# Gated DeltaNet heads: u and w no longer formed, each scan step solves with the transposed chunk inverse; decays in one orientation from rounded pairs

## The reference

```
G = cumsum(g);  decay[i,j] = exp(G_i - G_j) for i >= j
A = strictly_lower((beta k) k^T * decay)
u = (I + A)^-1 (v * beta);   w = (I + A)^-1 (k * beta * exp(G))
qk = (q k^T) * decay;  k_dec = k * exp(G_last - G)
for each chunk:
    v_new = u - w S
    o = (q exp(G)) S + qk v_new
    S = S * exp(G_last) + k_dec^T v_new
```

## Time and profile before

| | us |
|---|---|
| median of 3 runs | 2143.46 |
| lowest, highest | 2142.41, 2148.03 |
| span of the profiled execution | 2142.6 |

### The profile page before, as it was taken

How to read it: one execution, slowest core, us unless ns; L and a number is a source line. 1 busy time by engine, 2 the same in 40 slices (tenths; PEclk the granted TensorE clock), 3 DMA queues, 4 the chain that set the end, 5 groups by cost and what they waited for, 6 DMA issues and landing times. The chain is left out here.

```text
span 2142.6 us, 40127 instructions
## 1 busy us (share of the span) xinstructions
PE 1958.1 (91%) x15035; PEld 1587.5 (74%) x15036; DVE 1106.7 (52%) x1759; ACT 770.8 (36%) x1255; POOL 422.2 (20%) x332
## 2 busy tenths in 40 slices
PE   6899999999999989999999989899998998899990
PEld 3888888888886558887788866777776776677770
DVE  3446656656656464322322348555457557554338
ACT  2523423423432112221222202554446546543332
POOL 0154144245144031221111233100000000000004
PEclk7999999999999999999999999999999999999995
DMA  8042242243233532234322513875658758755354
GB/s 287 30 142 72 76 142 85 71 134 97 84 111 116 185 119 98 89 101 131 99 98 94 190 49 128 307 257 167 203 178 300 234 175 309 239 166 167 105 177 162
DMA packets 186864, 320.12 MB, mean 149 GB/s; under 512 B 26137, under 2 KB 77729, under 8 KB 186619
## 3 DMA queue, kind: packets, MB, share of 16 engines
q1 hardware_dynamic: 170683, 286.00, 40.8%
q10 hardware_dynamic: 12192, 17.00, 2.3%
q0 software_dynamic: 3744, 13.63, 1.8%
HBM read 283.89 MB, written 32.67 MB: 148 GB/s over the span
## 5 line engine op out<-in xcount | busy, mean ns | idle before, releaser
L1216 PE MATMUL pp<-whi,xTh 128*128 128x512 f32 (+1 forms) x1152 | 443.5, 385 | 22.4 <-issue 12.4
L1910 ACT ACTIVATE whi<-wring 128x1024 fp32r<-128x1024 f32 (+1 forms) x324 | 314.7, 979 | 411.2 <-PE pp L1218 353.6
L1218 PE MATMUL pp<-wlo,xTh 128*128 128x512 f32 (+1 forms) x1152 | 430.7, 374 | 0.0
L1217 PE MATMUL pp<-whi,xTl 128*128 128x512 f32 (+1 forms) x1152 | 429.9, 373 | 0.0
L2536 DVE TENSOR_TENSOR wlo<-wring,whi 128x1024 fp32r<-128x1024 f32 (+1 forms) x180 | 209.5, 1164 | 270.8 <-ACT whi L1910 222.7
L1216 PEld LDWEIGHTS pp<-whi,xTh 128*128 128x128 f32 x1152 | 218.0, 189 | 70.9 <-issue 27.8
L1218 PEld LDWEIGHTS pp<-wlo,xTh 128*128 128x128 f32 x1152 | 217.5, 189 | 38.9
L1217 PEld LDWEIGHTS pp<-whi,xTl 128*128 128x128 f32 x1152 | 218.3, 190 | 34.6
L1216 PE MATMUL pp<-whi,hTh 128*128 128x512 f32 x528 | 212.7, 403 | 7.8 <-DVE hTl L2558 2.8
L1218 PE MATMUL pp<-wlo,hTh 128*128 128x512 f32 x528 | 207.0, 392 | 0.0
L1217 PE MATMUL pp<-whi,hTl 128*128 128x512 f32 x528 | 206.6, 391 | 0.0
(11 more groups left out here) (321 smaller groups left out, 3065.5 us busy)
## 6 DMA issues: line engine op xcount, KB each, us to landing
wring<-in_moe_w_gu SPq DMA_DIRECT2D x320, 256.0 KB, 3.8
wring<-in_ada_w SPq DMA_DIRECT2D x80, 512.0 KB, 4.9
wring<-in_moe_w_down SPq DMA_DIRECT2D x160, 256.0 KB, 3.5
wring<-in_ffn_w_gu SPq DMA_DIRECT2D x80, 256.0 KB, 3.0
wring<-in_dn_w_in SPq DMA_DIRECT2D x128, 128.0 KB, 3.1
wring<-in_ffn_w_down SPq DMA_DIRECT2D x40, 256.0 KB, 2.9
expert_in<-zeros SPq DMA_DIRECT2D x36, 256.0 KB, 3.3
wring<-in_ada_w SPq DMA_DIRECT2D x32, 256.0 KB, 5.3
```

The costliest lines, as they stand in the source:

```text
L1216: pe.matmul(out, hi[:, c0 + c, tt], wh, start=(first and c == 0), stop=False)
L1217: pe.matmul(out, lo[:, c0 + c, tt], wh, start=False, stop=False)
L1218: mm = pe.matmul(out, hi[:, c0 + c, tt], wl, start=False, stop=(last and c == nk - 1))
L1910: act.activation(whi[:, hs, 0:nk, 0:w], wring[:, ring_v.slot(k), 2 * s:2 * s + nk, 0:w], ACT.Copy)\
```

## The change

u and w are no longer formed. With X = (I + A)^-1 diag(beta), a step is now: right side v - exp(G) (k S) on DVE (`right_sides`), solve X times that on PE (`solve`, one f32 product for each direction), copy to `vnew` on ACT (`new_values`), then the adds as before. beta goes into the decay (the bias of Exp) of the transposed A and into the decayed keys (`EKB`), so POOL's right sides go. Step 0 solves with v itself, and `reads` multiplies the transposed keys `kT` (two buffers now) with the state. Direction d uses `xinv[:, 1 - d]`.

The decays of both uses now come from one product in one orientation: the gates are split into a rounded high and a low part (`g_high`, `G_LOW`), POOL masks both (`span_high`, `span_low`, four operations instead of two), and PE multiplies them with a strict triangle in fp32r, 384 and 256 columns, high and low each, summed in PSUM. One Exp with log beta serves both A and the weights: `decay_w` and its Exp go, and `weights` waits for the blocks of A. At level 5 of the inverse half of the x products are not needed, and the inverse is kept as `xinv` instead of transposed.

The order changes on every engine. In the new scan the decays of head h + 1 come first (ACT's Exps before `new_values(1)` and behind it), then keys and Gram products, and the Silu of q and v between `new_values` 2, 3 and 4; before, ACT had the Silus first and the Exps behind them. On DVE the taps of the v convolution are spread over the steps. In POOL's block the causal weights, decayed keys and masks move among the level masks. Ahead of head 0 ACT does the Exps right behind the Silu of q. The core of the diff, without renamed buffers and semaphore counts:

```diff
 # PE
-            def decay_a(h, d): ...
-            def decay_w(h, d): ...
+            def decay(h, i):
+                if h == 0 and i == 0:
+                    pe.wait_ge(S["mask_ready"], 2)
+                    pe.wait_ge(S["gate_act"], 6)
+                pe.wait_ge(S["gm_ready"], 4 * h + 2 * i + 2)
+                if i:
+                    pe.wait_ge(S["qkn"], h + 1)
+                for part in (slice(0, 3 * P), slice(3 * P, NT)):
+                    out = PP[3 - i][:, part] if part.start == 0 else PP[3 - i][:, 512:512 + NT - 3 * P]
+                    pe.matmul(out, strict_mask[:, i, :], span_high[:, i, part], start=True, stop=False)
+                    mm = pe.matmul(out, strict_mask[:, i, :], span_low[:, i, part], start=False, stop=True)
+                mm.then_inc(S["decay_ps"], 1)
...
-                    for b in range(2):
+                    for b in ((1, 0) if n == 10 else (0, 1)):
                         for d in range(2):
                             p = halves(b)
+                            if n == 10 and b == d:
+                                continue
...
+            def solve(h, k):
+                for d in range(2):
+                    t = tile_of(k, d)
+                    if k == 0:
+                        pe.wait_ge(S["v_ready"], h + 1)
+                        pe.wait_ge(S["inv_upd"], h * 24 + upd_count(13 - d))
+                    else:
+                        pe.wait_ge(S["rhs_ready"], h * 8 + (2 * (k - 1) + d + 1))
+                        pe.wait_ge(S["o_upd"], h * 18 + 4 * (k - 1) + (4 if k == 1 else 2))
+                    if k == 1:
+                        pe.wait_ge(S["sp_ready"], h * 2 + (d + 1))
+                    pe.matmul(add_bank(d)[:, 2 * P:3 * P], xinv[:, 1 - d, t, :], rhs[:, d, :] if k else v_of(h)[:, tiles(t)],
+                              start=True, stop=True).then_inc(S["solve_ps"], 1)
...
 # scan(h) on PE now, in order (early: output units of the last head; the rest of h + 1 only if there is one)
+  solve(h, 0)   reads(h, 1)   early(0, 1)   decay(h + 1, 0)    adds(h, 0)   early(1, 2)
+  solve(h, 1)   early(2, 3)   decay(h + 1, 1)   adds(h, 1)     early(3, 4)
+  k_columns(h + 1)   reads(h, 2)   early(4, 5)   solve(h, 2)   early(5, 6)
+  gram_k(h + 1)      adds(h, 2)    early(6, 7)   reads(h, 3)   early(7, 8)
+  gram_q(h + 1)      solve(h, 3)   early(8, 9)   adds(h, 3)    early(9, 10)
+  v_tokens(h + 1)    reads(h, 4)   early(10, 11) solve(h, 4)   early(11, 12)   adds(h, 4)
 # ahead of head 0 on PE now
+  project(0, 24, 27)  decay(0, 0)  decay(0, 1)  project(0, 27, 29)  k_columns(0)  project(0, 29, 30)
+  gram_k(0)  project(0, 30, 32)  gram_q(0)  v_tokens(0)
 # POOL
-                for d, m in enumerate((GT, LT)):
-                    pool.tensor_tensor(per_tile(gm[:, d, :]), mat_bc(m), col_bc(gcol(G_, d, h)), ALU.mult)\
+                for i, m in enumerate((GE, LE)):
+                    for dst, col in ((span_high, g_high[...].bitcast(F32)), (span_low, gcol(G_LOW, 1 - i, h))):
+                        pool.tensor_tensor(per_tile(dst[:, i, :]), mat_bc(m), col_bc(col), ALU.mult)\
...
 # ACT
+            def decays(h, i):
+                act.wait_ge(S["decay_ps"], 2 * h + i + 1)
+                if h and i == 0:
+                    act.wait_ge(S["wm_step"], 2 * h)
+                d = 1 - i
                 for t in range(T):
+                    at = t * P if t < 3 else 512 + (t - 3) * P
+                    ins = act.activation(ex[:, i, t * P:(t + 1) * P], PP[3 - i][:, at:at + P], ACT.Exp,
                                          bias=gates5[:, LB, t, h + 8 * d:h + 8 * d + 1])
...
+                def new_values(k):
+                    for d in range(2):
+                        act.wait_ge(S["solve_ps"], h * 10 + (2 * k + d + 1))
+                        if h or k:
+                            act.wait_ge(S["s_add_ps"], h * 10 + 2 * (k - 1) + (d + 1))
+                        act.activation(vnew[:, d, :], add_bank(d)[:, 2 * P:3 * P], ACT.Copy).then_inc(S["vn_ready"], 1)
 # scan(h) on ACT now, in order
+  k_squares(h + 1)  new_values(0)  state_new of both d  decays(h + 1, 0)  new_values(1)  store of the state
+  decays(h + 1, 1)  k_columns(h + 1)  new_values(2)  grams(h + 1, 0)  conv_silu(h + 1, 1)  new_values(3)
+  grams(h + 1, 1)  conv_silu(h + 1, 2)  new_values(4)  v_tokens(h + 1)  q_squares(h + 1)  chunk_high  out_square(h)
 # ahead of head 0 on ACT now
+  k_squares(0)  conv_silu(0, 1)  decays(0, 0)  decays(0, 1)  k_columns(0)  grams(0, 0)  conv_silu(0, 2)  grams(0, 1)
+  z_silu(0)  v_tokens(0)  q_squares(0)
 # DVE
+                        dve.scalar_tensor_tensor(rhs[:, d, :], read_bank(d)[:, 0:P], gates5[:, MINUS_EG, t, h + 8 * d:h + 8 * d + 1],
+                                                 v_of(h)[:, tt], ALU.mult, ALU.add).then_inc(S["rhs_ready"], 1)
 # scan(h) on DVE now, in order; right_sides(k) also scales q S, conv(a) is tap a of v of head h + 1
+  k_sums(h + 1)  right_sides(1)  outputs(0)  k_normal(h + 1)  conv(0)  new_states(1)  outputs(1)  conv(1)
+  right_sides(2)  conv(2)  new_states(2)  outputs(2)  conv(3)  right_sides(3)  a_blocks(h + 1, 0)
+  new_states(3)  outputs(3)  conv(4)  right_sides(4)  a_blocks(h + 1, 1)  outputs(4)
```

More of the change, by code:

```diff
@@ L211, in backbone @@
         scratch = sb("scratch", [P, 15388])
+        strict_mask = sb("strict_mask", [P, 2, P], F32R)
+        g_high = sb("g_high", [P, T, 16], F32R)
         ctx.close()
@@ L1066, in scan @@
-                pe.wait_ge(S["kdec_ready"], h * 2 + 2)
-                pe.wait_ge(S["wm_step"], h * 2 + 2)
-                pe.wait_ge(S["wt_sb"], h * 2 + 2)
-                adds(h, 0)
-                early(0, 2)
+                solve(h, 0)
+                reads(h, 1)
+                early(0, 1)
+                if nx:
+                    decay(h + 1, 0)
+                adds(h, 0)
+                early(1, 2)
+                solve(h, 1)
+                early(2, 3)
+                if nx:
+                    decay(h + 1, 1)
@@ L1071, in scan @@
+                adds(h, 1)
+                early(3, 4)
                 if nx:
                     k_columns(h + 1)
-                reads(h, 1)
-                early(2, 3)
+                reads(h, 2)
+                early(4, 5)
+                solve(h, 2)
+                early(5, 6)
                 if nx:
                     gram_k(h + 1)
-                adds(h, 1)
-                early(3, 5)
+                adds(h, 2)
+                early(6, 7)
+                reads(h, 3)
+                early(7, 8)
@@ L1527, in _ @@
                     k_decayed(h, d)
+                for n in range(8, 10):
+                    off_mask(h, n)
                 for n in range(10, 12):
@@ L1841, in scan @@
                     act.wait_ge(S["state_out"], h * 32 + 1)
-                    act.activation(state_new[:, d, :], bank(2 * d + 1)[:, 0:P], ACT.Copy).then_inc(S["sp_ready"], 1)
+                    act.activation(state_new[:, d, :], add_bank(d)[:, 0:P], ACT.Copy).then_inc(S["sp_ready"], 1)
+                if nx:
+                    decays(h + 1, 0)
+                new_values(1)
                 for d in range(2):
@@ L2396, in scan, with outputs @@
+                def outputs(k):
+                    for d in range(2):
+                        t = tile_of(k, d)
+                        tt = slice(t * P, (t + 1) * P)
+                        out = add_bank(d)[:, P:2 * P]
                         dve.wait_ge(S["s_add_ps"], h * 10 + (2 * k + d + 1))
@@ L2417, in scan @@
-                    if nx and k == 0:
-                        conv(h + 1, 2, 2, 5)
-                assert n_o == 18
+                            dve.wait_ge(S["o_upd"], h * 18 + done[0])
+                            o_step(dve.tensor_tensor(oacc[:, tt], oacc[:, tt], out, ALU.add))
+                if nx:
+                    k_sums(h + 1)
+                right_sides(1)
+                outputs(0)
+                if nx:
+                    k_normal(h + 1)
+                if nx:
+                    conv(h + 1, 2, 0, 1)
@@ L2421, in _ @@
+                if nx:
+                    conv(h + 1, 2, 4, 5)
+                right_sides(4)
+                if nx:
+                    a_blocks(h + 1, 1)
+                outputs(4)
+                assert done[0] == 18
             for part in range(2):
```

373 lines of the change are left out of this document (168 added, 205 removed).

## The result

The changed kernel takes 2153.78 us (median, 2147.57 to 2162.93) against 2142.55 us (2137.57 to 2148.03) of the kernel before on the same chip: ratio 1.0056, interval 1.0044 to 1.0069. It is slower by 0.56%, 12 us; the prediction said 2135. The profiled execution has a span of 2148.2 us against 2142.6.

A forecast was written before the change was run, and what follows sets the result against it. PE, busy 91%, was first suspect, but in the scan the chain through DVE and ACT queues was to decide. 2142.6 - 8.5 - 2 - 3 = 2129.1 of span, 2130 as median; clock falls of 5 made 2135, range 2120 to 2150.

The forecast's parts named there:

- part 1: PE work in a scan falls by 5.6 us to 15.1, with both decays taking 1.2 us.
- more than 1.2: Sign that the prediction is wrong: the decays take more than 1.2 us on PE.
- Nothing: Inversion: the level 5 and POOL changes cost or gain nothing, since PE's filler covers them.
- part 2: Scan: the lengthened chain returns PE's lost work as gaps; 0.3 us gained instead of 5.6, -2 over seven scans.
- ±7: Seven scans: uncertainty of hand-overs, -1 to +1 us a scan, -7 to +7 in all.
- part 3: Set-up ahead of head 0 gains 8.5 us through the new ACT order; the last scan gains 3.
- part 4: Clock falls in four of seven scans, by the gap before the value transposes, at 1.2 us each: +5.
- a scan over 26.5 us: Sign that the prediction is wrong: L835 to L825 of a scan takes over 26.5 us; 24.3 was forecast.
- many long falls: Rival: clock falls in six heads at 2.4 us each, 14 us, giving 2144; chance 0.20.
- by it all seven heads would fall: Reading of the skill's clock page: PE waits in every scan, so the clock falls in all seven heads.

The follow-up runs named there:

- e4: Kernel before, with the second orientation of the decays computed for one tile of five on PE; 2143.1 us, ratio 0.9996.
- e12: Kernel before, with the 512-column decay product and four of five row-form decay tiles left out on PE; 2190.4 us, scan 23.67 us.
- e3: Changed kernel with POOL's causal weights put back ahead of the last two level masks; 2149.2 us, ratio 1.0030.
- e7: Changed kernel with idle-time products in PE's waits before the step 1 solve, the second Gram product and the value transposes; 2141.9 us, ratio 1.0004.
- e2: Changed kernel with the next head's value transposes moved behind the last solve on PE; 2131.7 us, ratio 0.9945.
- e5: Changed kernel with ACT's Silu of q moved to right behind the first new_values; 2156.2 us, ratio 1.0069.
- e1: Changed kernel with idle-time products on PE, two before the second Gram product and five before the value transposes; 2152.0 us, ratio 1.0033.
- e9: Changed kernel with two idle-time products on PE before the solve of step 1 and nothing else; 2158.1 us, ratio 1.0049.

## Why the prediction was wrong, point by point

- **PE work that goes (part 1): right.** The four products of a decay follow each other from 400.79 to 401.46, 0.67 us; for both that is 1.3 (1.2 said; the sign "more than 1.2" came true by 0.1 us). The time in which PE stands in the old scan is 3.9 us by my own figures (24.6 less 20.7), not about 3. e4 confirms that the work was worth next to nothing where it stood; e12 puts a size on the rest.
- **"Nothing" for the inversion: wrong by 0.38 us each, +2.2 in six.** I named PE's filler as the cover and did not ask what a moved POOL operation would meet on DVE. e3 undoes exactly this.
- **The chain laid over head 3 (part 2): right in its places, short in its size.** Waits of 1.21, 0.80, 2.60 and 0.51 us are where 1.57, 1.1, 2.8 and the last were said, with the releasers named. From the start of the scan, adds(0) ends at 3.9 us (3.7 said), adds(1) starts at 7.3 (7.1), adds(2) ends at 13.1 (12.7), the transposes start at 21.0 (20.3), and the scan ends at 25.14 (24.3). The error grows from 0.2 to 0.8 us over the scan. Part of it is read in the rows: the first f32 product behind a wait takes 0.32 us to the next (405.76 to 406.08), the others 0.22. I had given each hand-over its latency and none this restart. Against before, that is +0.49 us a scan instead of -0.3: +3.4 in seven instead of -2, inside the ±7 that I gave. That the restart is the whole 0.8 us was not tested.
- **Set-up and last scan (part 3): right in kind, and in the set-up's number partly by luck.** Set-up and head 0's inversion gave 8.8 where 8.5 was said. The query sums of head 0 start at 98.7 (100.9 said), 9.6 us earlier instead of 7.4; but the clock, which I had given a chance to stay up, fell right behind them, and the inversion took 56.6 us instead of 55.7. The two misses nearly cancel. ACT loads its table three times between 84 and 99 us; I had said four. Its rows, which answer to the earlier trace rows:

```profile
84.38 1.28 ACT L1725 ACT_TABLE_LOAD   x1
...
86.43 1.28 ACT L1763 ACT_TABLE_LOAD   x1
87.73 2.69 ACT L1763 ACTIVATE scratch<-pp,gates 128x128 f32<-128x128 f32 x10
...
93.77 1.28 ACT L1725 ACT_TABLE_LOAD   x1
```

  The last head gives 5.8, but about 3 of it is the fall that before happens to have there (5.84 us of PE work at half the clock, so an estimate of 2.9 lost); 3 was said.
- **The clock (part 4): the step that failed.** I wrote four falls of 1.2 us, +5. In after's profile there are seven in the scans and one in an inversion: the scans take 8.3 us more than seven of 25.14, and the sixth inversion 3.1 more than 54.02, +11.4 there. e7 prices it at 11 to 12 us in the median. I had looked only at the longest wait, before the transposes. Two of after's seven, and all five of e2, come at another place: 1.21 us before the solve of step 1, solve and decay, and 0.43 us more before adds(1). The sign "a scan over 26.5 us" came true in three heads (26.82, 28.00, 26.51), in each by falls. No rival of mine had the place of the first two waits; "many long falls" (2144) had the right mechanism and was still 10 us short, as it stood on the too short scan and on a cost-free inversion.

The parts against the profiled span of before: -8.8 set-up, +3.4 scans, +2.2 inversions, +11.4 clock in the heads, -5.8 last head, +3.1 behind it; unrounded they make 2148.2 - 2142.6 = 5.6. My terms made -8.5: -8.5 set-up, -2 scans, 0, +5 clock, -3 last head, 0. So of the 14 us between them the clock is 6.4, the undisturbed scans 5.4, the inversions 2.2 and the unchanged rest 3.1, less 3.1 for set-up and last head. The clock is the largest single miss, but it is not the whole: without the 11.4 us of falls in the heads, after's profile would lie about 6 us below before's, not the 13 of my sum. The medians differ by 11.2; the profiled execution of after is among its faster ones, and the falls differ from run to run: its runs spread over 15 us, those of before over 10, in line with falls that are a matter of luck in each scan, though the rest of the program varies as well. What was forecast as faster was the schedule without falls, and e7 puts even that at no difference, since its executions are not free of falls either.

Both pages of the Trainium skill can be set against the rows now. TensorE: Matmul & The Clock Gate, section "HAM oscillation", has a loop that leaves PE waiting lose its clock in every round: after falls in six of seven scans, e5 in all seven, e2 in five, e12, with a wait of 1.67 us, in one, and e4, with 1.73 us, in none. So the traces agree in kind, not for every loop that waits. The page's loop stands for 3 to 5 us in every round, longer than any wait here (2.6 us), so my "by it all seven heads would fall" went beyond what the page states. By that reading, at my 1.2 us each, the estimate would have been 2130 + 7 x 1.2 = 2138, nearer, but not near. ScalarE: Activation LUTs, section "What ACT_TABLE_LOAD costs", gives about 2.66 us for a switch, of which about 1.28 us is the load and 1.38 us a drain. The load agrees with the trace of after, 1.28 us; the drain does not show, as the first activation starts 0.01 to 0.02 us behind the load (86.43 and 87.73) and the load 0.02 us behind the activation ahead of it, so this chain pays about half of the page's figure.

## What to carry to other kernels

Work taken from an engine that shares a stage with a chain is worth only what it does on the chain, and the hole it leaves is a risk: lay the chain with all its queues over the old times, then list every hole on TensorE, not the longest alone. Look at what stands behind a wait in its in-order queue: the value transposes held up reads that did not need them, and moving that one call was worth 24 us, twice the loss, while removing a wait that only lengthens the next one (e5) was worth nothing. In the changed schedule, idle-time products in both of its long holes kept the clock in the profiled scans; in one place of two they gave little or nothing.

## What the runs showed of the hardware

- The price of falls: seven stretches of 3.4 or 6.8 us at half the clock in scans of 25 us and one right behind a scan go together with 11 to 12 us in the median, with the same schedule and nothing but idle-time products between the two kernels (after against e7). A single 3.4 us fall some 7.5 us into a scan costs 1.17 us (e2: 24.33 against 23.16; e1: 26.32 against 25.15); one 20 to 22 us into it costs that scan 0.5 to 1.4 us (e9: 25.65 to 26.51 against 25.14).
- Where a POOL and a DVE operation, both on SBUF, run side by side, both take longer: DVE's split of 128x1024 takes 2.26 us instead of 1.22, its tap of 128x644 1.42 instead of 0.88, while DVE's 128x320 updates that read PSUM keep their 0.49 us. POOL's two masks of 128x320 take 3.13 us together there and 1.70 alone.
- The first f32 product behind a wait takes 0.32 us to its successor instead of 0.22.
